# The scan's output summed in one PSUM bank: the state's product accumulates, tile by tile, onto the product of the scores

## The chip, the cores and the metric

The kernel runs on one core of one Trainium2 chip. The metric is the time of one execution on the device, in microseconds; the median of three runs stands for a kernel. The profiles are of one execution each, and their times are counted from the start of its span.

## The reference

The reference is a small language model's three layers on 1024 positions of width 1024: a Hawk layer (gated linear recurrence), an RWKV-7 layer, and a hybrid of a convolution and a state space model. The change touches one part of the RWKV-7 layer, the scan over time:

```python
def step(S, inp):
    r_t, w_t, k_t, v_t, a_t, b_t = inp
    sa = jnp.einsum('bhvk,bhk->bhv', S, a_t)
    S = S * w_t[:, :, None, :] + sa[..., None] * b_t[:, :, None, :] + v_t[..., None] * k_t[:, :, None, :]
    y = jnp.einsum('bhvk,bhk->bhv', S, r_t)
    return S, y
_, y = lax.scan(step, S0, xs)
```

There are 16 heads of 64 channels. S is a state of 64x64 numbers for each head, and y, one row of 64 numbers for each head and step, is what the rest of the layer reads.

## The kernel before, in words

The scan isn't run step by step. The 1024 steps are cut into 16 chunks of 64 (`NC`, `CHUNK`), taken in 8 pairs (`PAIRS`). Within a chunk all steps are written as matrix products, and only the state goes from chunk to chunk. Heads lie two by two on the 128 partitions: index `m` counts eight tiles of 128 channels (`DT`), and `e` is the head in the tile, on partitions 0 to 63 or 64 to 127 (`half(e)`).

For every chunk `n` TensorE (`pe`) does, in this order of kinds: products of the scores (`score`), of the matrix to invert (`raw`), transposes (`in_time`), five levels of an inversion by doubling (`w_step` and `x_step`), two products without the state (`last`); then, with the state, `u_step` (or `w_beside_u`, which does `u_tile` beside a level of the inversion) and `state`. The work is interleaved by hand: while the pair `p` goes through its inversion, the pair before it goes through its state steps, and the pair after it through its scores. All engines run lists of instructions written out in full, each in its own fixed order, and wait for each other with semaphores.

`state(n)` has three parts, each with one matmul for each `m` and `e`, 16 matmuls with 64 columns:

- `S`, L2658: the chunk's contribution to the state. The contraction runs over all 128 partitions, and the output goes to the half `e` of the partitions (a tile of the array with 128 rows and 64 columns).
- `yu`, L2664: the part of the output that comes from within the chunk, `UV` times the masked scores `G`. It has the same shape, 128 rows by 64 columns.
- `ys`, L2670: the part of the output that comes from the state at the start of the chunk, `S` times `rt`. Contraction over the 64 partitions of the head, a tile of 64 rows by 64 columns.

An fp32 matmul leaves two records in the trace, so each of the three parts is 32 records for a chunk; below, a pair of records is the two heads `e` of one tile, which start within some 7 ns of each other.

The results go through a ring of four PSUM banks (`RING`), which is shared by all products except those of the inversion. `claim` gives out the turns in the order of the list, `place` says which bank a turn has, `enter` lets TensorE wait until the bank's last content has been read, and `out`/`gone` count these reads. Before the change `yu` and `ys` have a bank each. ScalarE (`act`) copies the bank of `ys` to the SBUF tile `ys` (L2762), then VectorE (`dve`) adds the bank of `yu` and `ys`, and writes the chunk's columns of `o` (L2887; the trace calls this buffer rw_o). After the last chunk the block ends for all engines together, and the next one begins with head sums over `o` (L2970).

Near the end of the kernel, in the hybrid layer, stands another loop that the prediction reads: `outputs`, L3740 and L3742, in which for each of eight groups one matmul with 128 rows is followed by two with 64 rows that accumulate onto it. It isn't changed.

Of the kernel before, what the change touches and what calls it, by code (L numbers as in the profile page):

```python
# [5 lines left out]
P = 128  # L6
# [3 lines left out]
DT = D // P  # L10
# [11 lines left out]
CHUNK = 64  # L22
# [52 lines left out]
def build(nc, A, out, stop=None, start=None):  # L75
    fp32, r32 = mybir.dt.float32, mybir.dt.float32r
    ALU, ACT = mybir.AluOpType, mybir.ActivationFunctionType
    ds = bass.ds
    ctx = ExitStack()
    with ctx:  # L80
# [7 lines left out]
        def sig(name):  # L88
            if name not in signals:
                signals[name] = Signal(name, *semaphores.pop(0))  # L90
                made_in[-1].append(name)
            return signals[name]
# [21 lines left out]
        class Arena:  # L114


            def __init__(self, name, kib, c):
                self.base = (nc.sbuf_base + 31) // 32 * 32
                sb(name, [P, kib * 256], fp32, c)

            def at(self, name, shape, dt, kib):
                return nc.alloc_sbuf_tensor_at(name, shape, dt, offset=self.base + int(kib * 1024))
# [39 lines left out]
        def after(name, n):  # L162

            s = sig(name)
            return s.sem, s.at(n)

        def tick(name, by=1):
            return sig(name).sem, by
# [1251 lines left out]
        class ScanRoom:  # L1420
# [3 lines left out]
            def __init__(self, at):  # L1424
                self.G = at("sc_G", [P, 4, 2, DT, P], fp32, 32)
                self.AV = at("sc_AV", [P, 2, DT, HEAD], fp32, 64)
                self.WA = at("sc_WA", [P, 2, DT, CHUNK], fp32, 68)
                self.ops = at("sc_ops", [P, DT, 5, 2 * CHUNK], fp32, 72)
                self.rt = at("sc_rt", [P, DT, 2 * CHUNK], fp32, 92)
                self.mask = at("sc_mask", [P, 2, CHUNK], fp32, 96)  # L1430
                self.level = at("sc_level", [P, 5, CHUNK], fp32, 96.5)
                self.first = at("sc_first", [P, 2, CHUNK], fp32, 97.75)
                self.eye = at("sc_eye", [P, CHUNK], fp32, 98.25)
                self.UV = at("sc_UV", [P, 4, 2, DT, HEAD], fp32, 98.5)
                self.XX = at("sc_XX", [P, 4, 2, DT, CHUNK], fp32, 114.5)
                self.NT = at("sc_NT", [P, 2, 3, DT, CHUNK], fp32, 130.5)
                self.Wt = at("sc_Wt", [P, 2, DT, CHUNK], fp32, 144.25)
                self.grown = at("sc_grown", [P, DT, HEAD], fp32, 148.25)
                self.ys = at("sc_ys", [P, DT, CHUNK], fp32, 150.25)
                self.BK = at("sc_BK", [P, 4, 2, DT, HEAD], fp32, 152.25)  # L1440
                self.S = at("sc_S", [P, 2, DT, HEAD], fp32, 176.25)
                self.Gx = at("sc_Gx", [P, 2, DT, CHUNK], fp32, 180.25)
# [958 lines left out]
        def rwkv_scan(QD, pc, o, room):  # L2401
# [8 lines left out]
            RING = 4  # L2410
            smask, slevel, sfirst, seye, ops, rt = room.mask, room.level, room.first, room.eye, room.ops, room.rt
            G, BK, UV, XX, Gx, NT, Wt = room.G, room.BK, room.UV, room.XX, room.Gx, room.NT, room.Wt
            AV, WA, S, grown, ys = room.AV, room.WA, room.S, room.grown, room.ys
            bank = [ps[b // 2][:, b % 2, :] for b in range(8)]
            eight = [b.rearrange("p (m t) -> p m t", m=DT) for b in bank]
            four = [b.rearrange("p (m t) -> p m t", m=4) for b in bank]
# [2 lines left out]
            def half(e):  # L2419
                return slice(e * HEAD, (e + 1) * HEAD)  # L2420
# [6 lines left out]
            def claim(key, by=1):  # L2427
                turn[key] = len(incs)
                incs.append(by)
# [15 lines left out]

            def claim_state(n):
                claim(("S", n))
                claim(("yu", n))
                claim(("ys", n))

            def claim_last(n):
                claim(("WA", n))
# [6 lines left out]
            for p in range(PAIRS + 1):  # L2459
                n0, n1 = 2 * p - 2, 2 * p + 2  # L2460
# [15 lines left out]
            def place(key):  # L2476
                return 4 + turn[key] % RING

            def used(t):
                return sum(incs[t % RING:t:RING])  # L2480

            def enter(pe, key):
                t = turn[key]
                if t >= RING:
                    pe.wait_ge(*after(f"ring_{t % RING}", used(t)))

            def out(key):
                return tick(f"ring_{turn[key] % RING}")

            def gone(key):  # L2490
                t = turn[key]
                return after(f"ring_{t % RING}", used(t) + incs[t])
# [4 lines left out]
            with nc.Block() as block:  # L2497
# [25 lines left out]
                def _(pe):  # L2523
# [128 lines left out]
                    def state(n):  # L2652
                        a = n % 2
                        pe.wait_ge(*gone(("U", n)))
                        enter(pe, ("S", n))
                        for m in range(DT):
                            for e in range(2):
                                mm = pe.matmul(eight[place(("S", n))][half(e), m, :], BK[:, n % 4, e, m, :], UV[:, n % 4, e, m, :],  # L2658
                                               start=True, stop=True)
                        mm.then_inc(*tick("pe_S"))  # L2660
                        enter(pe, ("yu", n))
                        for m in range(DT):
                            for e in range(2):
                                mm = pe.matmul(eight[place(("yu", n))][half(e), m, :], UV[:, n % 4, e, m, :],  # L2664
                                               G[:, n % 4, e, m, CHUNK:2 * CHUNK], start=True, stop=True)
                        enter(pe, ("ys", n))
                        pe.wait_ge(*after("rt_in", 16 * (n // 2 + 1)))
                        for m in range(DT):
                            for e in range(2):
                                mm = pe.matmul(eight[place(("ys", n))][half(e), m, :], S[half(e), a, m, :], rt[half(e), m, a * CHUNK:(a + 1) * CHUNK],  # L2670
                                               start=True, stop=True)
                        mm.then_inc(*tick("pe_y"))

                    for n in range(2):
# [3 lines left out]
                    for p in range(PAIRS + 1):  # L2678
                        pair, n0, n1 = (2 * p, 2 * p + 1), 2 * p - 2, 2 * p + 2
# [45 lines left out]
                def _(act):  # L2725
# [31 lines left out]

                    def y_out(n):
                        act.wait_ge(*after("pe_y", n + 1))
                        if n >= 1:  # L2760
                            act.wait_ge(*gone(("yu", n - 1)))
                        act.activation(ys[:, :, :], eight[place(("ys", n))], ACT.Copy).then_inc(*out(("ys", n)))  # L2762

                    for n in range(2):
                        bx_out(n)
# [3 lines left out]
                    for p in range(PAIRS + 1):  # L2769
                        pair, n0, n1 = (2 * p, 2 * p + 1), 2 * p - 2, 2 * p + 2  # L2770
# [67 lines left out]
                def _(dve):  # L2838
# [30 lines left out]
                    def u_out(n):  # L2869
                        dve.wait_ge(*after("pe_U", n + 1))  # L2870
                        dve.tensor_copy(UV[half(0), n % 4, 0, :, :], eight[place(("U", n))][half(0), :, :]).then_inc(*out(("U", n)))
# [9 lines left out]
                        dve.tensor_tensor(S[:, 1 - a, :, :], grown[:, :, :], pc[:, :, n:n + 1].to_broadcast([P, DT, HEAD]), ALU.mult)\  # L2881
                           .then_inc(*tick("sc_S"))

                    def y_out(n):
                        dve.wait_ge(*after("pe_y", n + 1))
                        dve.wait_ge(*gone(("ys", n)))
                        dve.tensor_tensor(o[:, :, n * CHUNK:(n + 1) * CHUNK], eight[place(("yu", n))], ys[:, :, :], ALU.add)\  # L2887
                           .then_inc(*out(("yu", n)))

                    dve.memset(S[:, 0, :, :], 0.0).then_inc(*tick("sc_S"))  # L2890
                    dve.wait_ge(*after("sc_const", 64))
                    for n in range(2):
# [2 lines left out]
                    for p in range(PAIRS + 1):  # L2895
                        pair, n0, n1 = (2 * p, 2 * p + 1), 2 * p - 2, 2 * p + 2
                        inner, before, ahead = p < PAIRS, p > 0, p < PAIRS - 1

                        def x_both(l):
                            if inner:  # L2900
                                for n in pair:
                                    x_out(n, l)
                        for z in range(2):
                            if before:
                                u_out(n0 + z)
                            x_both(z)
                            if before:
                                state_out(n0 + z)
                                y_out(n0 + z)
                        if ahead:  # L2910
                            score_out(n1)
                        x_both(2)
                        if ahead:
                            raw_out(n1)
                        x_both(3)
                        if ahead:
                            score_out(n1 + 1)
                            raw_out(n1 + 1)
                        x_both(4)
# [1102 lines left out]
```

## Time and profile before

| | |
|---|---|
| median of 3 runs | 4007.84 us (4007.68 to 4012.25) |
| the profiled execution | 4004.69 us, span 4002.9 us |
| TensorE busy | 3657.2 us, 91% of the span |
| VectorE busy | 2515.3 us, 63% |
| ScalarE busy | 1486.1 us, 37% |
| mean granted clock of TensorE | 0.966 of full |
| the part with the 16 passages of `state` | 1722.6 to 2131.5 us |

The busy share of an engine is the time in which it had an instruction in progress. Matmuls overlap each other in the array (64 columns take some 220 ns from start to end, while a new pair starts every 58 ns), so the pace is read from the starts of records and not from their lengths. In the timeline the first column is the start, the second the length of the merged records, and a number in square brackets is idle time of the engine before them with what ended it; "issue" there means that the engine waited for nothing that the profile shows. Records of instructions of one line are merged with their count (x32).

### The profile page before, as it was taken

The page shows a single profiled execution, that of the slowest core. Times are in us where ns is not written, and L with a number is a line of the kernel's source. Part 1 is how long each engine was busy: PE and PEld are TensorE (multiplying, and loading weights), DVE is VectorE, ACT ScalarE, POOL GpSimd, SP SyncE. Part 2 cuts the span into 40 slices and gives each one's busy share as a digit, 9 for nine tenths or more (in the row PEclk, how much of TensorE's full clock was granted, in tenths as well). Part 3 has the DMA queues.
Part 4 walks back from the last instruction along what each step waited for, and adds up shares of the span by engine and source line. Part 5 has one row for each costly group of instructions (what it writes and reads, how often), then busy time and mean ns, then how long its engine had stood idle before and what let it go on. Part 6 is the DMA issues. An engine that isn't in the chain of part 4 may idle for free. (4 is left out here: it accounts for less than half of the span.)

```text
span 4002.9 us, 66745 instructions
## 1 busy us (share of the span) xinstructions
PE 3657.2 (91%) x29564; PEld 2989.2 (75%) x29564; DVE 2515.3 (63%) x2223; ACT 1486.1 (37%) x1554; POOL 1173.9 (29%) x537
## 2 busy tenths in 40 slices
PE   8999999999989989677776999999998999998897
PEld 6778788878767766676774778887886888875675
DVE  5564766778657858443445567668867888827532
ACT  5554433344433358322225433334354222112412
POOL 1135444455412111233230444555531000000211
PEclk9999999999999999899998999999998999998898
DMA  2111223353121327522113123235312222222422
GB/s 95 48 43 60 84 95 112 107 199 122 58 93 69 134 82 233 182 67 91 54 37 111 48 95 103 95 140 186 108 56 91 80 80 79 74 100 67 147 100 100
DMA packets 189376, 392.74 MB, mean 98 GB/s; under 512 B 16208, under 2 KB 85072, under 8 KB 183312
## 3 DMA queue, kind: packets, MB, share of 16 engines
q1 hardware_dynamic: 150368, 311.91, 23.6%
q10 hardware_dynamic: 38720, 76.56, 5.2%
q8 instruction: 234, 3.83, 0.4%
q14 instruction: 54, 0.44, 0.0%
HBM read 277.79 MB, written 110.10 MB: 97 GB/s over the span
## 5 line engine op out<-in xcount | busy, mean ns | idle before, releaser
L3696 POOL MEMSET ssm_toep<- 128x4096 f32 x1 | 3.5, 3511 | 544.6 <-POOLq L3395 544.6
L3282 DVE SCALAR_TENSOR_TENSOR H<-hy_cu,par,H 128x1024 f32<-128x1024 f32 x120 | 153.5, 1279 | 0.0
L269 POOL TENSOR_TENSOR wlo1C<-fast_raw,whi1C 128x1024 fp32r<-128x1024 f32 (+1 forms) x40 | 112.5, 2813 | 111.6 <-ACT whi1C L259 111.6
L269 POOL TENSOR_TENSOR wlo0B<-fast_raw,whi0B 128x1024 fp32r<-128x1024 f32 (+1 forms) x40 | 112.0, 2799 | 107.5 <-ACT whi0B L259 107.5
L3282 DVE SCALAR_TENSOR_TENSOR hy_odd<-hy_cu,par,hy_odd 128x1024 f32<-128x1024 f32 x112 | 143.3, 1279 | 0.0
L269 POOL TENSOR_TENSOR wlo1A<-fast_raw,whi1A 128x1024 fp32r<-128x1024 f32 (+1 forms) x40 | 111.5, 2787 | 103.9 <-ACT whi1A L259 103.9
L269 POOL TENSOR_TENSOR wlo1B<-fast_raw,whi1B 128x1024 fp32r<-128x1024 f32 (+1 forms) x39 | 108.0, 2769 | 113.9 <-ACT whi1B L259 113.9
L269 POOL TENSOR_TENSOR wlo0A<-fast_raw,whi0A 128x1024 fp32r<-128x1024 f32 (+1 forms) x40 | 110.1, 2753 | 104.8 <-ACT whi0A L259 104.8
L1007 DVE TENSOR_TENSOR fast_xl<-fast_xr,fast_xh 128x2048 fp32r<-128x2048 f32 (+1 forms) x42 | 127.7, 3063 | 20.9 <-ACT fast_xh L848 20.9
L269 POOL TENSOR_TENSOR wlo0C<-fast_raw,whi0C 128x1024 fp32r<-128x1024 f32 (+1 forms) x39 | 108.0, 2769 | 105.9 <-ACT whi0C L259 105.9
L2808 POOL TENSOR_TENSOR sc_NT<-sc_Gx,sc_level 128x512 f32<-128x512 f32 x80 | 100.3, 1273 | 100.1 <-PE psA L2584 78.5
L942 DVE TENSOR_TENSOR fast_g<-fast_g,flow_rms 128x1024 f32<-128x1024 f32 x44 | 126.5, 2875 | 1.5
L2801 POOL TENSOR_TENSOR sc_XX<-sc_XX,sc_eye 128x512 f32<-128x512 f32 x32 | 39.9, 1268 | 235.6 <-DVE sc_XX L2854 235.6
L2866 DVE TENSOR_TENSOR sc_XX<-psA,sc_XX 128x512 f32<-128x512 f32 (+1 forms) x80 | 52.2, 686 | 90.0 <-PE psA L2612 80.6
L834 ACT ACTIVATE fast_g<-fast_g 128x1024 f32<-128x1024 f32 x44 | 46.6, 1059 | 127.4 <-DVE fast_g L942 127.4
L269 POOL TENSOR_TENSOR wlo0C<-wraw0A,whi0C 128x1024 fp32r<-128x1024 f32 (+1 forms) x16 | 37.4, 2337 | 185.7 <-ACT whi0C L259 185.7
L269 POOL TENSOR_TENSOR wlo0A<-wraw0A,whi0A 128x1024 fp32r<-128x1024 f32 (+2 forms) x15 | 33.1, 2210 | 194.6 <-ACT whi0A L259 194.6
L848 ACT ACTIVATE fast_xh<-fast_xr 128x2048 fp32r<-128x2048 f32 (+1 forms) x42 | 74.1, 1764 | 12.4 <-DMA fast_xr<-ffn_x 12.3
L2323 DVE SCALAR_TENSOR_TENSOR flow_rms<-flow_rms,hawk_room_b 128x1024 f32<-128x1024 f32 x10 | 12.3, 1225 | 102.0 <-ACT flow_rms L2162 102.0
L959 DVE TENSOR_TENSOR fast_g<-fast_g,fast_s 128x1024 f32<-128x1024 f32 x22 | 72.6, 3302 | 0.8
L269 POOL TENSOR_TENSOR wlo0B<-wraw0A,whi0B 128x1024 fp32r<-128x1024 f32 (+2 forms) x15 | 32.7, 2177 | 130.1 <-ACT whi0B L259 130.1
L2584 PE MATMUL psB<-sc_XX,sc_NT 64*64 64x64 f32 x1280 | 60.7, 237 | 9.3 <-issue 9.2
(1467 smaller groups left out, 12216.9 us busy)
## 6 DMA issues: line engine op xcount, KB each, us to landing
fast_raw<-ffn_in_dram SPq DMA_DIRECT2D x88, 512.0 KB, 3.7
fast_xr<-ffn_x SPq DMA_DIRECT2D x28, 1024.0 KB, 5.9
sc_ops<-rw_arbkv SPq DMA_DIRECT2D x15, 1280.0 KB, 5.8
fast_raw<-ffn_out_dram SPq DMA_DIRECT2D x32, 512.0 KB, 3.7
wraw1A<-hybrid_in_dram SPq DMA_DIRECT2D x24, 512.0 KB, 3.4
wraw1B<-hybrid_in_dram SPq DMA_DIRECT2D x24, 512.0 KB, 3.5
ffn_x<-fast_g ACTq DMA_DIRECT2D x22, 512.0 KB, 3.3
ffn_x<-fast_e ACTq DMA_DIRECT2D x22, 512.0 KB, 2.8
```

Of the source, the lines that this page charges most:

```text
L269: eng.tensor_tensor(self.slot(wlo, n), self.raw[n], self.slot(whi, n).bitcast(fp32), ALU.subtract)\
L834: act.activation(g[:, :, z, :], g[:, :, z, :], ACT.Silu).then_inc(*tick("q_silu"))
L848: act.activation(part(hx, v, i), part(lr, v, i), ACT.Copy).then_inc(*tick("x7_hi"))
L942: dve.tensor_tensor(g[:, :, h, :], g[:, :, h, :], wide(h), ALU.mult).then_inc(*tick("q_g"))
L959: dve.tensor_tensor(g[:, :, 1, :], g[:, :, 1, :], s[:, :, :], ALU.mult).then_inc(*tick("q_h"))
L1007: dve.tensor_tensor(part(lx, v, i), part(lr, v, i), part(hx, v, i).bitcast(fp32), ALU.subtract)\
L2323: dve.scalar_tensor_tensor(out=e, in0=e, scalar=1.0, in1=tz, op0=ALU.add, op1=ALU.mult)\
L2584: mm = pe.matmul(eight[2 * a][half(e), m, :], NT[half(1 - e), a, (5 * (n // 2) + l) % 3, m, :], XX[half(1 - e), n % 4, e, m, :], start=Tru ...
L2801: pl.tensor_tensor(XX[:, n % 4, e, :, :], XX[:, n % 4, e, :, :], by_m(seye[:, :]), ALU.add)\
L2808: pl.tensor_tensor(NT[:, n % 2, k % 3, :, :], Gx[:, n % 2, :, :], by_m(slevel[:, l, :]), ALU.mult)\
L2866: dve.tensor_tensor(XX[r, n % 4, e, :, :], eight[2 * a + e][r, :, :], XX[r, n % 4, e, :, :], ALU.add)\
L3282: op = dve.scalar_tensor_tensor(out=acc, in0=c[:, j:j + T], scalar=w, in1=acc, op0=ALU.mult, op1=ALU.add)
```

## The change

The matmuls of `yu` and `ys` go to one bank, `y`. The loop over the tiles is now a single one: for each `m` first the two matmuls of `yu` (start of an accumulation), then the two of `ys` (which add to it and end it). ScalarE writes the sum straight from the bank to `o`, and VectorE's part and the buffer `ys` are gone. A chunk claims three turns of the ring with its state, not four.

```diff
             def claim_state(n):
                 claim(("S", n))
-                claim(("yu", n))
-                claim(("ys", n))
+                claim(("y", n))
...
                         mm.then_inc(*tick("pe_S"))
-                        enter(pe, ("yu", n))
-                        for m in range(DT):
-                            for e in range(2):
-                                mm = pe.matmul(eight[place(("yu", n))][half(e), m, :], UV[:, n % 4, e, m, :],
-                                               G[:, n % 4, e, m, CHUNK:2 * CHUNK], start=True, stop=True)
-                        enter(pe, ("ys", n))
+                        enter(pe, ("y", n))
                         pe.wait_ge(*after("rt_in", 16 * (n // 2 + 1)))
                         for m in range(DT):
+                            y = eight[place(("y", n))][:, m, :]
                             for e in range(2):
-                                mm = pe.matmul(eight[place(("ys", n))][half(e), m, :], S[half(e), a, m, :], rt[half(e), m, a * CHUNK:(a + 1) * CHUNK],
-                                               start=True, stop=True)
+                                pe.matmul(y[half(e), :], UV[:, n % 4, e, m, :], G[:, n % 4, e, m, CHUNK:2 * CHUNK], start=True, stop=False)
+                            for e in range(2):
+                                mm = pe.matmul(y[half(e), :], S[half(e), a, m, :], rt[half(e), m, a * CHUNK:(a + 1) * CHUNK],
+                                               start=False, stop=True)
                         mm.then_inc(*tick("pe_y"))
...
                     def y_out(n):
                         act.wait_ge(*after("pe_y", n + 1))
-                        if n >= 1:
-                            act.wait_ge(*gone(("yu", n - 1)))
-                        act.activation(ys[:, :, :], eight[place(("ys", n))], ACT.Copy).then_inc(*out(("ys", n)))
+                        act.activation(o[:, :, n * CHUNK:(n + 1) * CHUNK], eight[place(("y", n))], ACT.Copy).then_inc(*out(("y", n)))
...
-                    def y_out(n):
-                        dve.wait_ge(*after("pe_y", n + 1))
-                        dve.wait_ge(*gone(("ys", n)))
-                        dve.tensor_tensor(o[:, :, n * CHUNK:(n + 1) * CHUNK], eight[place(("yu", n))], ys[:, :, :], ALU.add)\
-                           .then_inc(*out(("yu", n)))
...
                                 state_out(n0 + z)
-                                y_out(n0 + z)
```

The last two hunks are VectorE's. The allocation of the buffer `ys` goes too.

## Rows read from the trace of the kernel before

**Rows 1.** The page, busy time of each engine over the span

```profile
PE 3657.2 (91%) x29564; PEld 2989.2 (75%) x29564; DVE 2515.3 (63%) x2223; ACT 1486.1 (37%) x1554; POOL 1173.9 (29%) x537
```

**Rows 2.** Busy time in the window of the scan; then PEclk, DMA share, GB/s

```profile
1700.00:2132.00 432.00, 325.13 (x13673) 308.99 (x13666) 183.72 (x286) 113.46 (x201) 118.38 (x95) 0.95 0.18 59
```

**Rows 3.** The waits, 1650 to 2140 us: total, times, longest

```profile
ACT sc_ys L2762 <- PE psD L2670: 60.5, 10, 10.1
...
DVE rw_o L2887 <- ACT sc_ys L2762: 34.5, 16, 5.6
...
PE psB L2610 <- issue: 14.7, 10, 3.7
...
PE psB L2612 <- issue: 11.5, 7, 2.4
```

**Rows 4.** Timeline of TensorE, the first passage of `state`

```profile
1722.59 1.15 PE L2658 MATMUL psC<-sc_UV,sc_BK 128*64 128x64 f32 x32
1723.57 1.10 PE L2664 MATMUL psD<-sc_G,sc_UV 128*64 128x64 f32 x32
1724.61 1.02 PE L2670 MATMUL psD<-sc_rt,sc_S 64*64 64x64 f32 x27
1725.86 0.34 PE L2670 MATMUL psD<-sc_rt,sc_S 64*64 64x64 f32 x5 [0.23 <-issue]
```

**Rows 5.** Timeline, u_tile's matmuls, which all have 64 rows

```profile
2118.75 0.28 PE L2639 MATMUL psC<-sc_AV,sc_XX 64*64 64x64 f32 x4
2118.87 0.28 PE L2642 MATMUL psC<-sc_S,sc_WA 64*64 64x64 f32 x4
```

**Rows 6.** Timeline, last pair before and first records after a change of tile size

```profile
2123.60 0.23 PE L2664 MATMUL psD<-sc_G,sc_UV 128*64 128x64 f32 x2
2123.76 0.33 PE L2670 MATMUL psD<-sc_rt,sc_S 64*64 64x64 f32 x3
```

**Rows 7.** The same from 64 rows to 128

```profile
1854.49 0.22 PE L2612 MATMUL psB<-sc_Wt,sc_XX 64*64 64x64 f32 x1
1854.64 0.28 PE L2658 MATMUL psC<-sc_UV,sc_BK 128*64 128x64 f32 x2
```

**Rows 8.** Timeline of the hybrid layer's `outputs`, which alternates

```profile
3638.75 0.49 PE L3740 MATMUL psD<-ssm_toep,ssm_ut 128*128 128x128 f32 x2
3639.17 0.71 PE L3742 MATMUL psD<-ssm_cq,ssm_e 64*128 64x128 f32 x4
3639.81 0.49 PE L3740 MATMUL psD<-ssm_toep,ssm_ut 128*128 128x128 f32 x2
```

**Rows 9.** Busy time in windows that run from one stall's end to the next's

```profile
1881.54:1885.29 3.75, 3.24 (x127) 3.10 (x126) 2.85 (x5) 0.00 (x0) 0.00 (x0) 1.00 0.02 4
1885.29:1889.14 3.85, 3.01 (x128) 2.88 (x128) 2.11 (x4) 1.19 (x2) 0.59 (x1) 1.00 0.02 4
```

**Rows 10.** DMA queue of the instructions, 1878 to 1899 us: packets, MB, share

```profile
q8 instruction: 6, 0.10, 2.2%
```

**Rows 11.** Timeline of TensorE, the fifth passage of `state`

```profile
1842.21 1.10 PE L2664 MATMUL psD<-sc_G,sc_UV 128*64 128x64 f32 x30
1846.39 0.47 PE L2664 MATMUL psD<-sc_G,sc_UV 128*64 128x64 f32 x2 [3.09 <-issue]
```

**Rows 12.** VectorE's sum and ScalarE's copy: ns min/median/max, first and last start

```profile
L2762 ACT ACTIVATE sc_ys<-psD x10: 597/597/598, 1726.2 to 2130.8; 128x512 f32<-128x512 f32 x10
...
L2887 DVE TENSOR_TENSOR rw_o<-psD,sc_ys x10: 691/692/692, 1726.9 to 2131.5; 128x512 f32<-128x512 f32 x10
```

**Rows 13.** Timeline of all engines at the end of the scan

```profile
2130.77 0.60 ACT L2762 ACTIVATE sc_ys<-psD 128x512 f32<-128x512 f32 x1 [3.36 <-PE psD L2670]
2131.47 0.69 DVE L2887 TENSOR_TENSOR rw_o<-psD,sc_ys 128x512 f32<-128x512 f32 x1 [1.29 <-ACT sc_ys L2762]
...
2132.48 1.10 PE L2970 MATMUL psC<-rw_o,const 128*128 128x512 f32 x2 [1.76 <-PEq L2497]
```

**Rows 14.** Windows: `outputs` of the hybrid layer, and 3.4 us after a stall

```profile
3638.70:3647.10 8.40, 8.40 (x51) 6.51 (x48) 6.94 (x9) 1.02 (x1) 0.00 (x0) 1.00 0.01 2
...
1846.40:1849.80 3.40, 3.40 (x68) 3.28 (x72) 0.29 (x1) 0.60 (x1) 0.00 (x0) 0.51 0.02 5
```

More of the change, by code:

```diff
@@ L1438, in __init__ @@
                 self.grown = at("sc_grown", [P, DT, HEAD], fp32, 148.25)
-                self.ys = at("sc_ys", [P, DT, CHUNK], fp32, 150.25)
                 self.BK = at("sc_BK", [P, 4, 2, DT, HEAD], fp32, 152.25)
@@ L2412, in rwkv_scan @@
             G, BK, UV, XX, Gx, NT, Wt = room.G, room.BK, room.UV, room.XX, room.Gx, room.NT, room.Wt
-            AV, WA, S, grown, ys = room.AV, room.WA, room.S, room.grown, room.ys
+            AV, WA, S, grown = room.AV, room.WA, room.S, room.grown
             bank = [ps[b // 2][:, b % 2, :] for b in range(8)]
```

## The prediction

> **What bounds the kernel now.** The page comes first: TensorE is busy for 91% of the span [rows 1], the next engine for 63%, so over the whole kernel a change pays or costs on TensorE. The window of the scan asks the same question of the part that is changed: in 432 us TensorE is busy for 325, VectorE for 184 and ScalarE for 113 [rows 2]. So there TensorE is idle for a quarter of the time, and the waits say on whom it waits: on no engine. The engines that take part in the change wait for TensorE: ScalarE's copy for L2670 (60 us in ten waits, up to 10.1 each), and VectorE's sum for that copy (34.5 us) [rows 3]. TensorE's own waits are put down to "issue", that is, to nothing that the profile names; the two largest groups sum to 26 us, with single ones up to 3.7 us [rows 3].
>
> What ends these stalls can be read from a table of windows. From the end of one stall to the end of the next TensorE executes 127 or 128 matmuls, with as many weight loads, in 3.75 and 3.85 us [rows 9]. In the 21 us from 1878 to 1899 us the queue that carries instructions moved 6 packets, 0.10 MB, so some 16 KB each, one in about 3.5 to 3.8 us [rows 10]. So one packet comes for each block of 127 weight loads and 127 matmuls. I read it so: TensorE's instructions come in blocks, a block can't be had sooner than about 3.8 us after the one before it, and where TensorE has executed its block sooner, it stalls. In these stretches the code's supply sets the pace, and elsewhere TensorE's own pace does. This matters for the sum: time added to a block that ends in a stall is taken from the stall.
>
> The pace without a stall: four records of u_tile, all with 64 rows, start every 0.117 us (2118.75, 2118.87), 0.0292 us per record [rows 5]. This stream changes every four records from one line to another, which accumulates onto the same bank, and loses nothing by it.
>
> **What is removed.** VectorE loses 16 sums of 0.692 us, 11 us in all [rows 12]. It waited before each of them, and TensorE waits for none: the next user of the bank is a score product that comes after two more w_steps. I cost it at nothing, with the last one as the exception. There the copy starts at 2130.77 and the sum at 2131.47, runs for 0.69, and the next block's first matmul follows at 2132.48 [rows 13]. The new end is the copy's: 2131.47 + 0.69 - (2130.77 + 0.60) = 0.79 us earlier. Take 0.8 off.
>
> **What is moved to ScalarE.** Its 16 copies stay as they are in shape, 0.597 us each [rows 12], with another destination. Its wait for the sum of the chunk before is gone, and nothing was behind it. Nothing for this.
>
> **The ring.** A pair of chunks now claims 32 turns and not 34. u of a pair's second chunk takes the turn behind the last product and no longer that of u of the first, and the first score takes y's bank of the first chunk. All these banks were read out long before. Nothing, between 0 and, if a score had to wait for one copy in each of 7 pairs, 0.6 x 7 = 4 us more. TensorE's list loses one wait for a chunk and no matmul, so the blocks of code end nearly where they end now.
>
> **What TensorE does otherwise.** This is the term that decides. The number of matmuls is the same, but their order isn't: 16 of 128 rows, then 16 of 64 rows become two and two in turn. What a change between these tile sizes costs can be read before the change, since each passage has one on its way in and one in its middle. On the way out, the last pair of L2664 starts at 2123.60 and the first of L2670 at 2123.76 [rows 6]: 0.15 us (the two roundings leave 0.15 to 0.16), where a pair's pace is 0.058, so 0.10 lost. The way in is the same: 1854.49 to 1854.64 [rows 7]. The second pair then comes late too: from the first L2658 at 1722.59 to the first L2664 at 1723.57 are 0.98 us for 32 records that at the pace would take 0.93 [rows 4], so 0.05 more. A change costs 0.147 us in each of the 16 passages. In the middle of the passage the sum agrees: 1723.57 to 1724.61 is 1.04, 0.93 and 0.10 [rows 4].
>
> That a lone change costs as much as one of many is seen in the hybrid layer, where no wait stands between the lines and the size changes with every group [rows 8]. Two records of 128 rows take 0.42 us there (3638.75 to 3639.17), four of 64 rows 0.64 (to 3639.81): two records more cost 0.22, so one costs 0.11, and each group bears 0.20 on top. Those have 128 columns; ours, with 64, are the cheaper ones. The bounds are thus 0.147 and 0.20 for a change, and I take 0.147, the same lines' own.
>
> The Trainium skill states this against the change: in TensorEngine Tiling, Key Properties, a change of tiling mode drains TensorE, while a change of the tile alone does not. The trace agrees with both halves [rows 5 to 8]; the page gives no price.
>
> The sum: within a passage there is 1 change now, and there will be 15 (two for each of eight tiles, less one). 14 x 0.147 = 2.06 us for a chunk, and 16 x 2.06 = 33 us for the scan. The y part of a passage, 64 records, goes from about 2.0 to about 4.1 us.
>
> **What of it is hidden.** In the fifth passage a stall of 3.09 us idle stands after 30 of 64 records [rows 11]: the changes before it, 0.9 us, come out of the stall, and the rest, 1.2 us, is exposed. In the first one the stall stands after 59 records and has 0.23 us of idle time, 0.4 over the pace [rows 4]: 0.4 is hidden there, and 0.15 in the stall that follows. Going through the passages like this, the part before the next stall against that stall, gives between 0 and 1.6 us each, and 6.3 us over the sixteen; in about half of them the block ends without a stall and nothing is hidden. The bounds: 0, and 26 us if each passage hid as much as the best. I take 6. What is late next: after the passage TensorE goes on with the inversion, so the whole rest of the scan, and of the kernel, moves by what is exposed, about 1.7 us for a chunk.
>
> The Trainium skill would hide nothing: in Runtime: NRT & Kernel Launch, Instruction fetch mechanics, it calls the crossing of a 16 KiB boundary "mostly hidden", so there would be no stalls to take from and the sum would be 33 - 0.8. The trace disagrees, with a stall at nearly every block [rows 3, 9].
>
> The profiled execution took 4004.7 us (span 4002.9 and 1.8 around it); 4004.7 + 33 - 6 - 0.8 = 4031. The median of the runs lies 3.1 us above that execution, so 4034 as a median. 0.2% of this kernel, some 8 us, is about what a measurement can tell from no change.
>
> **The rivals.**
>
> *Nothing is hidden*, for instance because blocks end elsewhere in the new list: 4007.8 + 33 - 0.8 = 4040. For it speaks that half the passages have no stall behind them; against it the long stalls within passages. 12%.
>
> *Most is hidden.* If supply sets the pace more strictly than I read, each passage gives what the best did: 33 - 26 - 0.8 = 6, so 4014, and up to 4024 for half of it. Against it: the fifth passage, with the longest stall of all, still exposes 1.2 of its 2.06 us. 10%.
>
> *The clock falls.* The passage doubles in length with the same work. After the stall of 3.1 us the granted clock was 0.51 for 3.4 us, in which 68 records ran [rows 14] where the pace gives 116, a loss of 1.4 us. If every passage brought on such a stretch: 16 x 1.4 = 22 more, 4056. Against it: the hybrid layer's alternating stretch of 8.4 us ran at 1.00 [rows 14], though its wider matmuls fill more of it. 13%.
>
> *Not slower*: the 0.147 us belongs to the waits that stand at these two places (for the ring and for rt), and not to the size. Then 14 of the 15 new changes, which have no wait, are free, TensorE's time stays, and the earlier end leaves 4007. It decides if a change without a wait costs under 0.03 us (14 x 16 x 0.03 = 7). Against it: from L2658 to L2664 there is a wait too and no loss [rows 4], and the hybrid layer pays without waits [rows 8]. 8%. That the freed VectorE lets something start sooner, and makes the kernel faster by over 8 us, would need a TensorE wait on VectorE that isn't in the trace: 2%.
>
> **How the numbers follow.** My forecast, partly hidden (4026 to 4040), has 55%. The 10% for most hidden lie between 4014 and 4026, the clock's between 4040 and 4056. The range from 4020 to 4050 leaves out the 10% not slower and some 8% at the two ends. A change at the hybrid layer's price of 0.20 would give 4034 + 14 x 16 x 0.053 = 4046, inside. Slower 0.90, same 0.08, faster 0.02.
>
> **What the profile after would show.** The passage from the first y matmul to the last some 4.1 us long in place of 2.0, rows of four records of each size in turn with some 0.26 us from one to the next; stalls behind and within them shorter; VectorE 11 us less busy; the window from the first passage to the last start of ScalarE's copy longer by some 26 us, and the rest of the kernel the same. Wrong would make me: groups that follow at 0.12 us (the size is free), a granted clock under 0.9 in the scan, or stalls that shrink by more than 10 us in sum.

## The result, and the profile after

The changed kernel is slower: 4035.7 us against 4010.1 (medians of four runs each), a ratio of 1.0066 with a 95% interval from 1.0053 to 1.0078, which is 26 us (21 to 31). The forecast was 4034, and a chance of 0.90 for slower. The profiled execution took 4036.95 us with a span of 4035.1; that of before took 4004.7, which is 5 us under the median of its kernel, so the two profiles lie 32 us apart and the medians 26.

The window of the scan after, from 1700 us to just behind the last passage, as all such windows below (busy time of TensorE, its weight loads, VectorE, ScalarE, GpSimd, with counts; then granted clock, DMA share, GB/s):

```profile
1700.00:2162.00 462.00, 363.38 (x13698) 331.04 (x13691) 172.95 (x272) 114.15 (x202) 118.38 (x95) 0.94 0.17 55
```

Beside [rows 2], the scan is 30 us longer (462 against 432). TensorE is busy for 38 us more with the same matmuls, and idle for 99 us in place of 107. VectorE has 11 us less, ScalarE what it had. The granted clock is 0.94, after 0.95.

The timeline of TensorE, the y part of the first passage, which answers to [rows 4]:

```profile
1723.69 0.29 PE L2664 MATMUL psD<-sc_G,sc_UV 128*64 128x64 f32 x4
1723.90 0.33 PE L2666 MATMUL psD<-sc_rt,sc_S 64*64 64x64 f32 x4
1724.16 0.34 PE L2664 MATMUL psD<-sc_G,sc_UV 128*64 128x64 f32 x4
1724.43 0.33 PE L2666 MATMUL psD<-sc_rt,sc_S 64*64 64x64 f32 x4
```

Read the starts, not the lengths. The first group of four follows records of its own size, so that only the second one, 0.21 us behind it, comes after a change of size. From then on each four records begin 0.26 or 0.27 us after the four before them. Four records of u_tile, which alternate between two lines as well, but with one tile size, begin 0.117 us after each other [rows 5]. So each group bears 0.147 us.

The end of the scan, timeline of all engines, which answers to [rows 13]:

```profile
2160.44 0.60 ACT L2756 ACTIVATE rw_o<-psD 128x512 f32<-128x512 f32 x1 [5.41 <-PE psD L2666]
...
2161.35 1.10 PE L2957 MATMUL psC<-rw_o,const 128*128 128x512 f32 x1 [0.95 <-PEq L2495]
```

From the last copy's start to the next block's first matmul are 0.91 us, after 1.71 before: the 0.8 us that were taken off.

### The profile page after: what moved, and what is told of

It reads as the page before. It is cut to its first block and busy times, and to the rows that moved or that the text cites. A ratio compares the mean times of both kernels' runs of the same rounds, so it can differ in the third digit from the quotient of the medians.

```text
span 4035.1 us, 66698 instructions
## 1 busy us (share of the span) xinstructions
PE 3698.0 (92%) x29564; PEld 3011.9 (75%) x29564; DVE 2504.7 (62%) x2207; ACT 1485.2 (37%) x1554; POOL 1171.9 (29%) x537
```

## The experiments

Each kernel was timed beside the kernel before on the same chip: the first four on one chip, and four_tiles_in_turn, the two halves and state_product_beside_w on another. The differences in us are the ratio's times 4010. Where a bank holds an accumulation that isn't finished tile by tile, only the first matmul of each half of the partitions opens the bank (`start=True` for `m == 0`), and the other tiles find it open. The Trainium skill says why, in PSUM — Partial Sum Buffer, The four PSUM rules: a matmul that opens an accumulation clears the marks of the whole bank on the quarters of the partitions that it writes, so that a later opening would make the first tile's second product overwrite and not add. No run here shows this, as none opened a bank twice under an unfinished sum.

**Which property of the new order costs the time: accumulation, alternation, or the size?** Three kernels, each with one property changed.

In order, in one bank:

```diff
-                        for m in range(DT):
-                            y = eight[place(("y", n))][:, m, :]
+                        y = eight[place(("y", n))]
+                        for q in range(0, DT, 8):
+                            for m in range(q, q + 8):
                                 for e in range(2):
-                                pe.matmul(y[half(e), :], UV..., G..., start=True, stop=False)
+                                    pe.matmul(y[half(e), m, :], UV..., G..., start=(m == 0), stop=False)
+                            for m in range(q, q + 8):
                                 for e in range(2):
-                                mm = pe.matmul(y[half(e), :], S..., rt..., start=False, stop=True)
+                                    mm = pe.matmul(y[half(e), m, :], S..., rt..., start=False, stop=(m == DT - 1))
```

> The changed kernel with the order of before: all 16 matmuls of yu, then all 16 of ys, accumulating in one bank (only the first matmul of each half of the partitions opens the bank); ScalarE still writes the sum. Theory (each change of the tile size costs 0.147 us): one change within the passage as before, y part of a passage 1.96 us without a stall, time of the kernel before less 0.8 us for the shorter end, so 0 to 2 us below it. Rival (accumulation in a bank onto products just written costs the time): still some of the 25 us, as the accumulation is still there, 5 us or more above the kernel before. Rival (ScalarE's copy or the ring's new turns cost it): the full 25 us.

Measured: ratio 0.9999 (0.9990 to 1.0008), -0.4 us. The timeline of its last passage:

```profile
2135.08 1.10 PE L2665 MATMUL psD<-sc_G,sc_UV 128*64 128x64 f32 x32
2136.11 1.15 PE L2669 MATMUL psD<-sc_rt,sc_S 64*64 64x64 f32 x32
```

From the first group to the second 1.03 us, as in [rows 4]. With accumulation, ScalarE's direct copy and the new turns of the ring, and without alternation, the 26 us are gone. That rules out both rivals.

Alternating, in two banks without accumulation (the kernel before, with its two loops over `m` made one; both waits now stand ahead of it):

```diff
                         enter(pe, ("yu", n))
-                        for m in range(DT):
-                            for e in range(2):
-                                mm = pe.matmul(eight[place(("yu", n))]..., start=True, stop=True)
                         enter(pe, ("ys", n))
                         pe.wait_ge(*after("rt_in", 16 * (n // 2 + 1)))
                         for m in range(DT):
+                            for e in range(2):
+                                mm = pe.matmul(eight[place(("yu", n))]..., start=True, stop=True)
                             for e in range(2):
                                 mm = pe.matmul(eight[place(("ys", n))]..., start=True, stop=True)
```

> The kernel before with one thing changed: the matmuls of yu and ys alternate tile by tile as in the changed kernel, but in two banks, without accumulation, and VectorE still adds. Theory: 15 changes of the tile size in a passage, the y part 4.0 us long, 26 us above the kernel before. Rival (accumulation costs it): as the kernel before, within 2 us, the y part 2.0 us.

Measured: ratio 1.0059 (1.0047 to 1.0072), +24 us (19 to 29). Its timeline has the starts of the changed kernel, 0.26 or 0.27 apart:

```profile
2144.87 0.34 PE L2666 MATMUL psD<-sc_G,sc_UV 128*64 128x64 f32 x4
2145.14 0.33 PE L2669 MATMUL psD<-sc_rt,sc_S 64*64 64x64 f32 x4
2145.40 0.34 PE L2666 MATMUL psD<-sc_G,sc_UV 128*64 128x64 f32 x4
```

So the order alone brings the loss, without a product added to another.

Alternating and accumulating, with one tile size. The state's product gets 128 rows, with a copy `Sz` of the state that has zeros where the other head's rows are. VectorE sets it to zero once, ScalarE fills it after each chunk, and TensorE waits for that (neither the zeroing nor the wait is shown):

```diff
-                                mm = pe.matmul(y[half(e), :], S[half(e), a, m, :], rt[half(e), m, a * CHUNK:(a + 1) * CHUNK],
+                                mm = pe.matmul(y[half(e), :], Sz[:, e, m, :], rt[:, m, a * CHUNK:(a + 1) * CHUNK],
                                                start=False, stop=True)
...
+                        if n < NC - 1:
+                            act.wait_ge(*after("sc_S", n + 2))
+                            for e in range(2):
+                                act.activation(Sz[half(e), e, :, :], S[half(e), (n + 1) % 2, :, :], ACT.Copy).then_inc(*tick("sc_Sz"))
```

> The changed kernel, tile by tile in one bank with accumulation, but ys has 128 rows too: its stationary operand is the state of one head with zeros for the other head's partitions (two more copies of 64 partitions by ScalarE for each chunk, some 19 us of ScalarE in all). So the order alternates and accumulates, and the tile size stays. Theory: no change of size within the passage, the y part 1.87 us (64 records at 0.0292), kernel within 2 us of the kernel before. Rival (accumulation or alternation by itself costs it): y part 4.0 us, 25 us above the kernel before.

Measured: ratio 0.9998 (0.9989 to 1.0007), -0.8 us. Its timeline:

```profile
2128.43 0.29 PE L2666 MATMUL psD<-sc_G,sc_UV 128*64 128x64 f32 x4
2128.55 0.29 PE L2668 MATMUL psD<-sc_rt,sc_Sz 128*64 128x64 f32 x4
2128.66 0.29 PE L2666 MATMUL psD<-sc_G,sc_UV 128*64 128x64 f32 x4
2128.78 0.29 PE L2668 MATMUL psD<-sc_rt,sc_Sz 128*64 128x64 f32 x4
```

This is the same interleaving, tile by tile and added up in one bank, and each four records start 0.117 us after the last four. Of what TensorE does, the tile's size differs from the changed kernel, and with it the state's product reads all 128 partitions of `rt`. The extra copies on ScalarE, shown in the groups by line, bring no loss that the times show:

```profile
L2762 ACT ACTIVATE sc_Sz<-sc_S 64x512 f32<-64x512 f32 x30 | 18.8, 628 | 0.7
```

**How the loss grows with the number of changes.** The in-order kernel with two tiles in turn, then with four (`range(0, DT, 2)` and `q + 2`; 4 for 2):

> The changed kernel with two tiles in turn: eight records of 128 rows, then eight of 64, so 7 changes of size in a passage instead of 15. Theory, by the dose: 6 x 0.147 = 0.88 us more than before for a passage (y part 2.85 us), 14 us in the scan, of which 3 to 5 are hidden by stalls for code: 9 to 11 us above the kernel before. Rival (the clock falls with long passages and takes part of the 25 us): under 8 us, since these passages are short. Rival (accumulation): the same 25 us as the changed kernel.

> One bank, four tiles in turn: 3 changes of size in a passage, 2 more than in order. By the dose 2 x 0.147 x 16 = 4.7 us more on TensorE (passage 2.3 us). Two tiles in turn had 14 us more by this count and 5 us more in time, one tile in turn 33 and 26: so what the stalls take comes first, up to about 8 us. Theory: within 2 us of the kernel before. Rival (a fixed share of each change is hidden): 4.7 x 26/33 = 3.7 us above.

Measured: two tiles in turn 1.0013 (1.0005 to 1.0022), +5.2 us (2 to 9); four 1.0002 (0.9993 to 1.0010), +0.8 us (-3 to 4). The timeline of the first of them:

```profile
2139.65 0.45 PE L2669 MATMUL psD<-sc_rt,sc_S 64*64 64x64 f32 x8
2140.03 0.45 PE L2665 MATMUL psD<-sc_G,sc_UV 128*64 128x64 f32 x8
2140.41 0.45 PE L2669 MATMUL psD<-sc_rt,sc_S 64*64 64x64 f32 x8
```

Eight records take 0.38 us, of which 8 x 0.0292 = 0.234 is the pace: 0.147 for a change again. The passages without a stall grow by just that: from the first y record's start to the last one's are 1.96 us in order, 2.26 with four tiles in turn, 2.84 with two and 4.02 with one. With the price of one change fixed, the table shows what reaches the end. The kernels with one bank also have the 0.8 us of the earlier end, which their added time is less by:

| changes in a passage | added on TensorE (0.147 each, 16 passages), less the earlier end | measured | not seen at the end |
|---|---|---|---|
| 1 (in order) | 0 less 0.8 | -0.4 | |
| 3 (four tiles in turn) | 4.7 less 0.8 | +0.8 | 3 |
| 7 (two tiles) | 14.1 less 0.8 | +5.2 | 8 |
| 15 (one tile, two banks) | 32.9 | +24 | 9 |
| 15 (one tile, the changed kernel) | 32.9 less 0.8 | +26 | 6 |

Each measured number has a margin of 3 to 5 us. If a fixed share of each change were hidden, as in the kernels with 15 changes, two tiles in turn would cost 9.5 to 10.6 us; their interval ends at 8.8. So it is likely that the first microseconds are swallowed and the later ones less. My expectation for two tiles, 9 to 11, was too high, and its hidden share, 3 to 5 us, too low. The four-tile result lies within its margin of both theories for it (2 and 3.7).

**Does the place decide what is hidden?** Tile by tile in eight chunks, in order in the other eight (`g = 1 if n in (...) else DT`), once where the trace of before had stalls behind the passage, and once where it hadn't:

> One bank; tile by tile in the chunks 0, 2, 4, 5, 6, 7, 9, 11, in order (all yu, then all ys) in the other eight. In the trace of before these are the passages that have a stall for code in or right behind them: 5.9 us of their 16.5 us were reckoned hidden. Theory: 16.5 - 5.9 = 10.6 us above the kernel in order. Rival (nothing is hidden by stalls): 16.5 us above, and the same as the other half.

> The complement: tile by tile in the chunks 1, 3, 8, 10, 12 to 15, of whose 16.5 us only 0.4 were reckoned hidden. Theory: 16.1 us above the kernel in order, 5 us more than the other half. Rival (each passage is hidden alike, because the code is supplied evenly): both halves within 2 us of each other, near 12 to 13 us.

Measured: the covered half 1.0021 (1.0011 to 1.0031), +8.4 us (4 to 12); the bare half 1.0037 (1.0024 to 1.0049), +14.8 us (10 to 20). Both have the same number of changes. The first forecast was 10.6 us above the kernel in order and the second 16.1; measured are 8.8 and 15.2 above it. Windows, in order first, then the covered half, then the bare one, each to just behind its last passage:

```profile
1700.00:2138.00 438.00, 323.43 (x13669) 306.98 (x13664) 172.50 (x270) 113.50 (x201) 118.38 (x95) 0.96 0.18 58
```

```profile
1700.00:2151.00 451.00, 347.39 (x13726) 323.54 (x13727) 174.10 (x274) 114.08 (x202) 118.43 (x95) 0.94 0.17 56
```

```profile
1700.00:2157.00 457.00, 347.06 (x13726) 321.49 (x13723) 173.25 (x272) 113.70 (x202) 118.35 (x95) 0.94 0.17 56
```

TensorE's busy time rises alike, to 347. Its idle time is 114.6 us in order (438 - 323.4), 103.6 in the covered half and 109.9 in the bare one. The 6 us between the two halves are what was reckoned from the trace of before (5.5), but neither view shows it firmly. The ratios lie 6.4 us apart with intervals that overlap, and the medians only 3. The windows come from one execution each, and that of the bare half was the slowest of its five (4030.9, with a median of 4025.2). Idle time also differs by 8 us between executions of kernels that take equally long, as the table further down has it. That the place decides is likely, and not shown.

**Is TensorE's own pace the bound of the scan at all?** The other way round: take work from TensorE without taking instructions. The state's product runs beside the next step of the inversion, as u_tile does.

```diff
+                    def w_beside_y(n, l, k):
+                        w_ready(n, l)
+                        for m in range(DT):
+                            y = y_tile(k, m)
+                            w = w_tile(n, l, m)
+                            if m == DT - 1:
+                                y.then_inc(*tick("pe_y"))
+                        w.then_inc(*tick("pe_W"))
...
-                        w_both(2)
+                        if inner and before:
+                            w_beside_y(pair[0], 2, n0 + 1)
+                            w_step(pair[1], 2)
+                        else:
+                            w_both(2)
```

> One bank, in order, but the 16 matmuls of ys run tile by tile beside the next step of the inversion (w_step), whose matmuls take the other two quarters of the array, for the 14 chunks where there is one. Both have 64 rows, so no change of size is added, and TensorE's own work gets 0.93 us shorter for a chunk, 13 us in all. Theory (code supply sets the pace in the blocks that end in a stall): most of it goes into longer stalls, 0 to 4 us below the kernel before. Rival (TensorE's own pace is the bound of the scan): 10 to 13 us below.

Measured: ratio 0.9992 (0.9983 to 1.0000), -3.2 us (-7 to 0). The timeline shows the two lines side by side, two records of each every 0.06 us, where each alone would have taken that:

```profile
2093.91 0.22 PE L2673 MATMUL psD<-sc_rt,sc_S 64*64 64x64 f32 x2
2093.92 0.23 PE L2582 MATMUL psA<-sc_XX,sc_NT 64*64 64x64 f32 x2
2093.96 0.23 PE L2673 MATMUL psD<-sc_rt,sc_S 64*64 64x64 f32 x2
```

And its window of the scan:

```profile
1700.00:2138.50 438.50, 317.86 (x13853) 300.30 (x13852) 175.76 (x274) 111.41 (x201) 118.37 (x95) 0.96 0.18 58
```

The scan took as long as in order. TensorE's busy time is 5.6 us lower than there and its idle time 6.0 higher, 120.6. That is less than the 13 us by which its work was to get shorter. Added up record by record (each takes only the time that no earlier one covers), the time of the state's product and of the inversion step of a pair's first chunk, which it runs beside, did fall, by 11 us; that of all others together rose by 5. A part of that is in the records themselves, since the traces miss some, and not equally many (13669 and 13853 are there). So the saving is real where it was made, and about 3 us of it came out at the end, with an interval that leaves out the rival's 10 to 13. This is the fastest kernel of the study, but at the edge of its own interval; as the kernel to keep I would name it only with more runs.

**Do the stalls wait for code?** The traces have the times of the queue that carries instructions, whose packets are of 16384 bytes. In the scan of before, from 1720 us, TensorE has 90 stalls of over 0.2 us. Of these 69 end 1.2 to 1.5 us after such a packet has landed, where the packets come 3.8 us apart in the median; by chance it would be one in twelve or so. After the change it is 62 of 79, and about 80 us of idle time end so in either kernel. The next packet's transfer begins 1.2 us (median) after TensorE has gone on and takes 1.0 us. These three parts make up most of the 3.8 us.

Windows of the scan side by side, with the profiled execution's time; the last column sums the stretches at the lower clock (half of full) in the trace's clock records:

| kernel | us of the execution | window | TensorE busy | idle | clock | at half speed |
|---|---|---|---|---|---|---|
| before | 4004.7 | 432 | 325.1 | 106.9 | 0.95 | 44 |
| in order | 4009.7 | 438 | 323.4 | 114.6 | 0.96 | 38 |
| one size | 4003.7 | 431 | 322.6 | 108.4 | 0.96 | 31 |
| two tiles | 4013.8 | 443 | 339.8 | 103.2 | 0.95 | 48 |
| two banks | 4029.9 | 458 | 361.0 | 97.0 | 0.94 | 51 |
| changed | 4037.0 | 462 | 363.4 | 98.6 | 0.94 | 55 |

## Why the prediction was right

*The bound.* TensorE sets the end and the other engines of the change wait for it. VectorE's 11 us and its wait were worth 0.8 us at the end of the scan, by the timelines, and nothing else that can be seen: the kernel in order has all of that gain and stands at -0.4 us, with an interval of 4 us on either side.

*The price of a change of tile size*, 0.147 us, read from two boundaries of each passage of before. It held in every new place: groups of four records at 0.264, of eight at 0.38. That it is the size, and not the alternation, the accumulation or the waits at those two places, was argued from [rows 5] and [rows 8]; it is shown now by the three kernels that take the properties apart.

*The count*, 14 more in each of 16 passages, 33 us. The y part of a passage without a stall went from 1.96 to 4.02 us, where about 4.1 were forecast.

*What is hidden.* 6 us were reckoned, and the times say 6 (33 added, 0.8 off at the end, 26 measured, with some 5 us of margin). That this number came out is in part luck, as it is what is left of two larger ones. The three kernels that take as long as before have a busy time of 324 us and an idle time of 110 in the mean, the two with 15 changes 362 and 98. So the stalls shrank by about 12 us and not by 6, and the busy time grew by some 38 and not by 33. By one pair of profiles, before and after, the stalls shrank by 8. The prediction named stalls that shrink by more than 10 us in sum as a sign of being wrong; between 8 and 12, with single executions that differ by 8, this sign is neither there nor absent. That the stalls are waits for blocks of code, and that added time is taken from them, was only read from the trace. The first half is borne out by the times of the instruction packets. For the second speak that the loss begins only after some microseconds of added work, that most of what was taken off TensorE did not come out at the end, and, less firmly, that the place of the added work matters.

*Where a size was off.* For two tiles in turn I forecast that 3 to 5 us would be hidden, and about 8 were. The shares of one passage had been reckoned for the full 2.06 us; with half as much in a passage more of it may lie ahead of the stall, which no run tested. In the fifth passage seven changes stand ahead of the stall, 1.03 us and not 0.9. And for *most is hidden* the number for half of the 26 us is 4027, not 4024. Neither moves the forecast.

*The clock.* The sum put it at nothing, and as a rival it was to bring 22 us, if each passage caused a slow stretch. The stretches at half speed sum to 31 to 44 us in the three kernels that take as long as before and to 51 and 55 in the two with 15 changes, some 15 us more in the mean. At the price of [rows 14], 1.4 us in 3.4, that is 6 us (an estimate), which is about the busy time beyond the 33. So the rival was right in kind and a quarter of its size; the larger shrinking of the stalls took its cost back. No run varied the clock by itself.

## What to carry to other kernels

Before matmuls are put in another order, write the rows of the array that each one uses beside it. Here two sorts of tile in turn cost a fixed time at every change, which two sorts one after the other pay once, and tiles of one size alternated and accumulated at full pace. If results have to be added up in one bank, the order needn't follow the sum: all first products, opened once, and then all second ones cost nothing here.

Where an engine has idle time that nothing explains, look whether it comes at equal numbers of instructions. If so, and if the instruction queue's packets land just ahead of where it goes on, small additions to that engine may be free, and small savings worth little.

## What the runs showed of the hardware

- A change between tiles of 128x64 and 64x64 costs 0.147 us at full clock, in both directions, whether a semaphore is waited for there or not. Two heads' matmuls in different halves of the array accumulate into one bank at the full pace of 0.058 us a pair.
- TensorE's instruction supply gave one block of 127 weight loads and 127 matmuls in about 3.8 us [rows 9]; at 0.0292 us each the matmuls of such a block need 3.7, and less where two products run side by side. The Trainium skill, in Runtime: NRT & Kernel Launch, Instruction fetch mechanics, calls the crossing of such a block's boundary mostly hidden. The traces disagree: TensorE was idle for 97 to 121 us of the 431 to 462 of the scan, and about 80 of them, before and after, ended just behind the landing of a block.
